# A hybrid diffusion step with top-2 experts: inner tile and position bias moved from TensorE to VectorE, block bounds read inside the blocks

## The chip, the cores and the metric

The kernel runs on one core of one Trainium2 chip. The time is the device time of one execution in microseconds. Before the change the median of three runs is 1415.07 us (1414.96 to 1417.32).

## The reference, cut to what matters

Two layers work on 128 context tokens and 256 latent tokens of width 1024. Layer 0 mixes tokens by differential attention, layer 1 by neighbourhood attention: each latent token sees 16 columns of 64 in the rows of its grid (4 rows here), with a learned bias by relative position, and all 128 context keys. After each attention every token goes through two of 32 experts, chosen by its own scores.

```python
s_nb = einsum('bqhd,biqjhd->bhqij', q_r, k_nb) * scale + bias      # layer 1, latent tokens
s = concatenate([s_nb.reshape(B, H, GRID_W, kh * kw), s_ctx], -1)
p = softmax(s, -1)
...
def one_block(args):                                               # experts, both layers
    tok, e, w = args
    xb = xt[tok]
    hb = silu(xb @ w_gate[e]) * (xb @ w_up[e])                     # 1024 -> 512
    return (hb @ w_down[e]) * w[:, None]                           # 512 -> 1024
```

## The kernel before

All is fp32. The order of the work on each engine is written out by hand, with semaphores between the engines.

**Experts.** Tokens are sorted into blocks of 32 of one expert each. The layers have 73 such blocks together (TensorE works on 77, the last ones of a layer being fillers). An expert's weights are six pieces of 1 MB: four of gate and up (pieces 0 to 3), two of down (4 and 5). The ring `ring` holds three experts. The SP queue (`load`, L361 to L384) loads expert after expert; from the fourth on, each piece waits until TensorE has read the piece of the expert three before it for the last time (`taken`: `gu_used`, `dn_used`), and until the same piece of the expert before has landed (`moe_land`).

A block with 32 tokens uses the array in four groups of 32 columns. In `gate_up` (L1072) group j takes the tokens as weights and, as moving data, columns j x 128 to j x 128 + 127 of w_gate and of w_up, so partition group j of the PSUM bank holds the hidden columns of that run for the 32 tokens, gate beside up (W = 256). ScalarE takes Silu of the gate half (`sg`, L755), VectorE multiplies by the up half (`hp`, L1555). For the down products the hidden index has to stand on partitions: TensorE transposes hp (128x128, L1090) to PSUM, and ScalarE copies it to `hm` (L758). In `down` (L1092) each of four 32-column pieces of hm is the weight for four column groups of w_down (WD = 256 columns each). VectorE copies the result to `yo` (L1563), and GpSimd stores it by an indirect DMA (L560). GpSimd also gathers the tokens of the block two ahead (L547) into `xg`, which VectorE turns into `xs` by its blockwise transpose (L1550), in every body after hp and ahead of the copy to yo.

TensorE's loop (L1106 to L1115) runs over triples of experts, with three inner loops over the blocks of one expert. Each inner loop's bounds, `first` and `end`, are read from the table `tabi` in SBUF into registers by `table` (L298) just ahead of it.

**Attention of layer 1.** A unit u is one tile of 128 queries and one pair of heads, 24 units, the first eight the context tile (128 keys, no bias), sixteen latent (384 keys: 128 context, 256 latent). `scores` (L905) puts both heads' scores into two PSUM banks; for latent units TensorE then adds the bias to the last 256 columns, by a product of the identity with the table `btab` (L919). VectorE's `maxima` (L1273) takes the negated maximum over all keys of both heads; ScalarE's `exps` (L695) takes the exponentials with that as bias and sums them; VectorE's `normalise` (L1316) divides; TensorE transposes the probabilities (L930); ScalarE copies these (`take_pT`, L708); TensorE multiplies by the values (`attend`, L934); VectorE takes the output (`take_oT`, L1325). TensorE's order in a turn is transposes of u, scores of u + 3, attend of u - 1; VectorE's is maxima of u + 1, normalise of u, output of u - 2; ScalarE's is exponentials of u + 2, copy of u. The mask of the 16-column window is added to btab by VectorE in twelve steps (L1267) while the projections run, and TensorE waits for the twelve ahead of its first transposes of this stage (L879).

## Time and profile before

| | us |
|---|---|
| median of the runs | 1415.07 |
| the profiled execution's own time | 1414.9 |
| its span, first to last instruction | 1413.1 |
| TensorE busy (matmul) | 1083.7 |
| VectorE busy | 401.0 |
| ScalarE busy | 180.4 |
| GpSimd busy | 255.4 |

The profile is of one execution on one core. Its times count from the start of the span. TensorE's matmuls are pipelined and their ends are modelled, so a following group can start up to 0.2 us before the one ahead of it ends; weight loads (PEld) run beside them. Reading registers from a table, branches and semaphores are not counted as busy. `[1.07 <-issue]` is idle time ended by nothing that the profile shows. PEclk is TensorE's granted clock: 1.00 is 2.4 GHz, 0.50 is 1.2 GHz. The mean granted clock over the span was 0.895.

The stages in the profile: layer 0's projections, attention and routing to about 378 us, its experts to 717, layer 1's projections to 886, its attention to 971, output projection, norm and routing to 1038, its experts to 1370.

### The profile page before, as it was taken

The page shows a single profiled execution, that of the slowest core. Times are in us where ns is not written, and L with a number is a line of the kernel's source. Part 1 is how long each engine was busy: PE and PEld are TensorE (multiplying, and loading weights), DVE is VectorE, ACT ScalarE, POOL GpSimd, SP SyncE. Part 2 cuts the span into 40 slices and gives each one's busy share as a digit, 9 for nine tenths or more (in the row PEclk, how much of TensorE's full clock was granted, in tenths as well). Part 3 has the DMA queues.
Part 4 walks back from the last instruction along what each step waited for, and adds up shares of the span by engine and source line. Part 5 has one row for each costly group of instructions (what it writes and reads, how often), then busy time and mean ns, then how long its engine had stood idle before and what let it go on. Part 6 is the DMA issues. An engine that isn't in the chain of part 4 may idle for free.

```text
span 1413.1 us, 26713 instructions
## 1 busy us (share of the span) xinstructions
PE 1083.7 (77%) x9857; PEld 561.9 (40%) x9858; DVE 401.0 (28%) x965; ACT 180.4 (13%) x485; POOL 255.4 (18%) x450
## 2 busy tenths in 40 slices
PE   5899998798687786656557999899837657788781
PEld 1333344544344443323223444565434323444440
DVE  0120217768411111001035002565871001111117
ACT  0110026400000000000012000552000000000000
POOL 2000002201133333212102010000022212333230
PEclk9999998897599999877787999899958878999996
DMA  9866892107979999999965993201079999999932
GB/s 367 305 239 262 332 358 86 60 18 257 415 319 387 414 415 414 415 415 416 416 267 126 113 160 117 75 1 60 30 298 413 412 415 417 415 379 389 414 112 109
DMA packets 85414, 389.76 MB, mean 276 GB/s; under 512 B 17612, under 2 KB 18124, under 8 KB 57720
## 3 DMA queue, kind: packets, MB, share of 16 engines
q1 hardware_dynamic: 63136, 349.77, 63.4%
q0 software_dynamic: 15200, 36.74, 9.6%
q10 hardware_dynamic: 7032, 2.68, 0.7%
q8 instruction: 24, 0.39, 0.1%
q14 instruction: 22, 0.18, 0.0%
HBM read 379.66 MB, written 17.44 MB: 281 GB/s over the span
## 4 chain that ended last, share of the span: by engine, by line
DMA 41%; PE 34%; issue 9%; DVE 9%; ACT 2%; DVEq 1%; POOLq 1%; SPq 1%; POOL 0%; ACTq 0%; PEldq 0%
DMA ring<-in_w_down_dram 36%; PE ps L824 15%; PE ps L1083 5%; PE ps L985 3%; PE ps L1101 3%; DMA ring<-in_w_ada_dram 2%; PE ps L800 1%; PE ps L930 1%; PE ps L912 1%; PE ps L919 1%; PE ps L952 1%; POOLq L457 1%; DVEq L1123 1%; DMA qkv<-ybuf 1%; DVE o L1201 1%
## 5 line engine op out<-in xcount | busy, mean ns | idle before, releaser
L1083 PE MATMUL ps<-ring,xs 128*32 128x256 f32 x4928 | 316.5, 411 | 115.0 <-DMA ring<-in_w_up_dram 75.1
L1083 PEld LDWEIGHTS ps<-ring,xs 128*32 128x32 f32 x4928 | 181.5, 117 | 242.7 <-issue 162.1
L824 PE MATMUL ps<-ring,hT 128*128 128x512 f32 x576 | 254.7, 601 | 8.1 <-ACT hT L648 4.3
L1101 PE MATMUL ps<-ring,hm 128*32 128x256 f32 x2464 | 158.7, 399 | 31.2 <-ACT hm L758 26.8
L824 PEld LDWEIGHTS ps<-ring,hT 128*128 128x128 f32 x576 | 109.6, 193 | 152.2 <-issue 141.9
L1555 DVE TENSOR_TENSOR hp<-sg,ps 128x128 f32<-128x128 f32 x73 | 21.0, 288 | 379.2 <-ACT sg L755 379.2
L1101 PEld LDWEIGHTS ps<-ring,hm 128*32 128x32 f32 x2464 | 73.6, 113 | 91.7 <-ACT hm L758 41.1
L547 POOL DMA_INDIRECT xg<-xmod,idx x77 | 80.8, 1050 | 66.0 <-POOL idx L545 63.9
L755 ACT ACTIVATE sg<-ps 128x128 f32<-128x128 f32 x73 | 20.2, 277 | 553.2 <-PE ps L1083 553.2
L560 POOL DMA_INDIRECT ybuf<-yo,idy x73 | 75.1, 1029 | 64.4 <-POOL idy L557 64.4
L985 PE MATMUL ps<-ring,qT 128*128 128x512 f32 x192 | 85.0, 603 | 2.2 <-DVE qT L1366 1.8
L1563 DVE COPY yo<-ps 128x256 f32<-128x256 f32 x73 | 31.0, 424 | 188.2 <-PE ps L1101 188.2
L557 POOL COPY idy<-rowi 128x1 int32 (+1 forms) x73 | 13.2, 181 | 344.7 <-DVE yo L1563 330.5
L800 PE MATMUL ps<-ring,cond 128*32 128x512 f32 x384 | 56.5, 707 | 17.5 <-DMA ring<-in_w_ada_dram 17.5
L1090 PE MATMUL ps<-cst,hp 128*128 128x128 f32 x77 | 25.9, 336 | 52.2 <-DVE hp L1555 50.7
L985 PEld LDWEIGHTS ps<-ring,qT 128*128 128x128 f32 x192 | 36.8, 194 | 47.9 <-issue 45.1
L704 ACT ACTIVATE hT<-ps,negm 128x384 f32<-128x384 f32 (+1 forms) x96 | 48.0, 505 | 54.5 <-DVE negm L1279 49.1
L1090 PEld LDWEIGHTS ps<-cst,hp 128*128 128x128 f32 x77 | 10.9, 141 | 91.9 <-DVE hp L1555 90.2
L686 ACT ACTIVATE qkv<-ps 128x1024 f32<-128x1024 f32 x18 | 18.4, 1023 | 220.4 <-PE ps L824 220.4
L912 PE MATMUL ps<-kT,qT 64*128 64x384 f32 (+1 forms) x192 | 42.3, 526 | 4.0 <-ACT hT L704 2.3
L930 PE MATMUL ps<-cst,hT 128*128 128x128 f32 x168 | 31.1, 304 | 12.1 <-DVE hT L1289 8.9
L1279 DVE TENSOR_REDUCE negm<-ps 128x2 f32<-128x768 f32 (+1 forms) x48 | 36.9, 773 | 4.5 <-PE ps L912 4.3
(269 smaller groups left out, 838.0 us busy)
## 6 DMA issues: line engine op xcount, KB each, us to landing
ring<-in_w_gate_dram SPq DMA_DIRECT2D x82, 1024.0 KB, 15.0
ring<-in_w_up_dram SPq DMA_DIRECT2D x82, 1024.0 KB, 15.5
ring<-in_w_down_dram SPq DMA_DIRECT2D x82, 1024.0 KB, 15.9
ring<-in_w_ada_dram SPq DMA_DIRECT2D x48, 1024.0 KB, 8.2
ring<-in_w_qkv_a_dram SPq DMA_DIRECT2D x12, 1024.0 KB, 5.3
ring<-in_w_qkv_b_dram SPq DMA_DIRECT2D x12, 1024.0 KB, 15.2
modb<-mdram POOLq DMA_DIRECT2D x12, 512.0 KB, 8.8
qkv<-ybuf SPq DMA_DIRECT2D x6, 1024.0 KB, 8.3
```

Of the source, the lines that this page charges most:

```text
L547: pool.indirect_dma_start(out=xg[:, lane, :], out_offset=None, in_=xmod.rearrange("r (j w) -> (r j) w", j=G), in_offset=bass.IndirectOffse ...
L560: pool.indirect_dma_start(out=ybuf.rearrange("r (j w) -> (r j) w", j=G), out_offset=bass.IndirectOffsetOnAxis(ap=at, axis=0), in_=yo[:, la ...
L704: ins = act.activation(e[:, h, 0:n], ps[:, 2 * (u % 2) + h, 0:n], ACT.Exp, bias=negm[:, u % 2, h:h + 1], accum_out=sums[:, t % 2, h, u % P ...
L800: ins = mm(ps[j * BLK:(j + 1) * BLK, ADA_BANK[i], :], cond[:, k, :], raw[:, n % RING, j * 512:(j + 1) * 512], start=(k == 0), stop=(k == K ...
L824: ins = mm(ps[:, 2 * t + hf, :], lhs[:, k, t * P:(t + 1) * P], raw[:, slot, kk * D + hf * 512:kk * D + (hf + 1) * 512], start=(k == 0), st ...
L912: ins = mm(ps[:, 2 * (u % 2) + h, 0:keys[t]], qT[HD * h:HD * (h + 1), j, t * P:(t + 1) * P], kT[HD * h:HD * (h + 1), j, key0[t]:key0[t] + ...
L930: ins = nc.tensor.transpose(ps[:, 4 + (u % 2 if l == 0 else h), i * P:(i + 1) * P], prob[u % 2][:, h, i * P:(i + 1) * P], ident)
L985: ins = mm(ps[:, 2 * t + hf, :], oT[:, k, t * P:(t + 1) * P], raw[:, n % RING, kk * D + hf * 512:kk * D + (hf + 1) * 512], start=(k == 0), ...
L1083: ins = mm(ps[j * BLK:(j + 1) * BLK, 1, 0:W].rearrange("p (a n) -> p a n", a=2), xs[:, k, :], w[:, :, at:at + FW], start=(k == 0), stop=(k ...
L1090: nc.tensor.transpose(ps[:, 3, 0:P], hp[:, :], ident).then_inc(ht_done[l], 1)
L1101: ins = mm(ps[j * BLK:(j + 1) * BLK, 5, 0:WD], hm[:, 2 * c + q, :], ring[:, slot + GU + c, q * D + j * WD:q * D + (j + 1) * WD], start=(c ...
L1279: v.tensor_reduce(negm[:, u % 2, :], sc[:, :, 0:n], AX, ALU.max, negate=True).then_inc(negm_rdy[l], 1)
```

## The change

1. In `gate_up` group j now takes, from each run of 128 columns (f = 0 to 3), the 32 columns f x 128 + 32 j onwards, of gate and of up, so the moving data are eight runs of 32 columns in place of two of 128. The products, their number and the columns per product stay. With this mapping the 128x128 tile hp needs only its sixteen 32x32 blocks turned, each in place, to be the hm of the down products. VectorE does that with its blockwise transpose from SBUF to SBUF, behind a drain. TensorE's transpose, ScalarE's copy and two semaphores go.
2. For latent units of layer 1 TensorE no longer adds the bias. `maxima` takes the maximum over the 128 context columns of both heads into `most`, then, for each head, one instruction adds the bias to the 256 latent columns in PSUM and takes their maximum together with that of the context columns; a small step negates both. Between these stand drains.
3. TensorE no longer waits for the masks; VectorE, which writes them, has a drain behind them.
4. The loop bounds of an expert are carried in registers: `lo` and `hi` are set before the loops, and in every block, between gate_up and down, the end of the next expert is read from the table into `after`. Behind an inner loop two register moves take the place of the two reads.

```diff
...
@@ -246,7 +247,7 @@
         idx_rdy, idy_rdy = sem2("idx_rdy"), sem2("idy_rdy")
         gath = [[sem(f"gath{l}_{i}") for i in range(LANES)] for l in range(LAYERS)]
         y_wr = [[sem(f"y_wr{l}_{i}") for i in range(LANES)] for l in range(LAYERS)]
-        xs_rdy, hp_rdy, ht_done, sg_rdy, hm_rdy = sem2("xs_rdy"), sem2("hp_rdy"), sem2("ht_done"), sem2("sg_rdy"), sem2("hm_rdy")
+        xs_rdy, sg_rdy, hm_rdy = sem2("xs_rdy"), sem2("sg_rdy"), sem2("hm_rdy")
         yo_rdy = sem2("yo_rdy")
         pool_steps, sp_steps = sem("pool_steps"), sem("sp_steps")
         sq_done, sq_rdy, hn_rdy = sem("sq_done"), sem("sq_rdy"), sem("hn_rdy")
...
@@ -754,16 +755,9 @@
                     act.wait_ge(gu_used[l], read_up(b))
                     act.activation(sg[:, :], ps[:, 1, 0:FW], ACT.Silu).then_inc(sg_rdy[l], 1)
-                    act.wait_ge(ht_done[l], b + 1)
-                    act.activation(hm[:, :, :], ps[:, 3, 0:P].rearrange("p (j n) -> p j n", j=G), ACT.Copy)\
-                        .then_inc(hm_rdy[l], 1)
-
                 body(0)
                 with act.Fori(1, n_blk) as b:
                     body(b)
-
-                act.wait_ge(dn_used[l], n_blk * 2 + 2)
-                act.sem_inc(hm_rdy[l], BUFS - 1)
                 for t in range(NT):
                     act.wait_ge(yg_ld[l][t], 16)
...
@@ -875,8 +871,6 @@
                 if l == 0:
                     pe.wait_ge(roped, 4)
                     pe.wait_ge(mblk_ev, 5)
-                else:
-                    pe.wait_ge(bias_rdy, 12)
                 pe.wait_ge(qkv_ev[l], 9)
                 pe.wait_ge(ctx_ld[l], 32)
                 for j in range(PAIRS):
...
@@ -907,17 +901,10 @@
                     if u >= 2:
                         pe.wait_ge(exp_done[l], u - 1)
-                    biased = l == 1 and t > 0
                     for h in range(2):
                         ins = mm(ps[:, 2 * (u % 2) + h, 0:keys[t]],
                                  qT[HD * h:HD * (h + 1), j, t * P:(t + 1) * P],
-                                 kT[HD * h:HD * (h + 1), j, key0[t]:key0[t] + keys[t]], start=True, stop=not biased)
-                    if biased:
-                        m0 = (2 - 2 * (t - 1)) * GRID_W
-                        for h in range(2):
-                            at = (2 * j + h) * BM * GRID_W + m0
-                            ins = mm(ps[:, 2 * (u % 2) + h, P:keys[t]], ident, btab[:, at:at + ROWS * GRID_W],
-                                     start=False, stop=True)
+                                 kT[HD * h:HD * (h + 1), j, key0[t]:key0[t] + keys[t]], start=True, stop=True)
                     ins.then_inc(sc_done[l], 1)
                 def transpose_prob(u):
...
@@ -1068,6 +1055,8 @@
                 pe.wait_ge(tab_rdy, l + 1)
                 pe.wait_ge(tok_rdy, l + 1)
                 n_trip = table(pe, T_TRIP, 1, (NE + BUFS) // BUFS)
+                pe.reg_mov(lo, 0)
+                pe.reg_mov(hi, table(pe, T_CUM + 2, 1, NB + BUFS - 1))
                 def gate_up(b, slot, landed):
...
@@ -1079,15 +1068,11 @@
                         for kk in range(4):
                             k = 4 * half + kk
                             for j in range(G):
-                                at = kk * DE + j * FW
-                                ins = mm(ps[j * BLK:(j + 1) * BLK, 1, 0:W].rearrange("p (a n) -> p a n", a=2), xs[:, k, :],
-                                         w[:, :, at:at + FW], start=(k == 0), stop=(k == KD - 1))
+                                ins = mm(ps[j * BLK:(j + 1) * BLK, 1, 0:W].rearrange("p (a f n) -> p a f n", a=2, f=G),
+                                         xs[:, k, :],
+                                         w[:, :, kk * DE:(kk + 1) * DE].rearrange("p a (f j n) -> p a f j n", f=G, j=G)
+                                         [:, :, :, j, :], start=(k == 0), stop=(k == KD - 1))
                         ins.then_inc(gu_used[l], 1)
-
-                def transpose_h(b):
-
-                    pe.wait_ge(hp_rdy[l], b + 1)
-                    nc.tensor.transpose(ps[:, 3, 0:P], hp[:, :], ident).then_inc(ht_done[l], 1)
                 def down(b, slot, landed):
...
@@ -1107,12 +1092,12 @@
                     for turn in range(BUFS):
                         at = trip * BUFS + turn
                         landed = at * 16 + 16
-                        first = table(pe, T_CUM + 1 + at, 0, NB)
-                        end = table(pe, T_CUM + 2 + at, 1, NB + BUFS - 1)
-                        with pe.Fori(first, end) as b:
+                        with pe.Fori(lo, hi) as b:
                             gate_up(b, BASE[turn], landed)
-                            transpose_h(b)
+                            pe.reg_mov(after, table(pe, T_CUM + 3 + at, 0, NB + BUFS - 1))
                             down(b, BASE[turn], landed)
+                        pe.reg_mov(lo, hi)
+                        pe.reg_mov(hi, after)
         @block.vector
         def _(dve):
...
@@ -1265,7 +1250,8 @@
                     for f in range(12):
                         part = btab[:, f * 512:(f + 1) * 512].rearrange("p (a n) -> p a n", n=GRID_W)
                         v.tensor_tensor(part, part, cst[:, C_WIN:C_WIN + GRID_W].unsqueeze(1).to_broadcast([P, 8, GRID_W]),
-                                        ALU.add).then_inc(bias_rdy, 1)
+                                        ALU.add)
+                    dve.drain()
                 for j in range(PAIRS):
                     dve.wait_ge(qk_ps[l], 2 * j + 2)
                     v.tensor_copy(kT[:, j, :], ps[:, 5 + 2 * (j % 2), :]).then_inc(kT_ev[l], 1)
...
@@ -1276,7 +1262,17 @@
                     n = keys[t]
                     sc = ps[:, 2 * (u % 2):2 * (u % 2) + 2, :]
                     dve.wait_ge(sc_done[l], u + 1)
-                    v.tensor_reduce(negm[:, u % 2, :], sc[:, :, 0:n], AX, ALU.max, negate=True).then_inc(negm_rdy[l], 1)
+                    if l == 0 or t == 0:
+                        v.tensor_reduce(negm[:, u % 2, :], sc[:, :, 0:n], AX, ALU.max, negate=True).then_inc(negm_rdy[l], 1)
+                        return
+                    m0 = (2 - 2 * (t - 1)) * GRID_W
+                    chain(v.tensor_reduce(most[:, 0:2], sc[:, :, 0:P], AX, ALU.max))
+                    for h in range(2):
+                        at = (2 * j + h) * BM * GRID_W + m0
+                        v.tensor_tensor_reduce(sc[:, h, P:n], sc[:, h, P:n], btab[:, at:at + ROWS * GRID_W], 1.0,
+                                               most[:, h:h + 1], ALU.add, ALU.max, most[:, 2 + h:3 + h])
+                    dve.drain()
+                    v.tensor_scalar(negm[:, u % 2, :], most[:, 2:4], -1.0, None, ALU.mult).then_inc(negm_rdy[l], 1)
                 def combine(u):
                     t, j = u // PAIRS, u % PAIRS
...
@@ -1552,7 +1548,8 @@
                 def hidden(b):
                     dve.wait_ge(sg_rdy[l], b + 1)
-                    v.tensor_tensor(hp[:, :], sg[:, :], ps[:, 1, FW:W], ALU.mult).then_inc(hp_rdy[l], 1)
+                    chain(v.tensor_tensor(hp[:, :], sg[:, :], ps[:, 1, FW:W], ALU.mult))
+                    v.transpose(hm[:, :, :].rearrange("p f n -> p (f n)"), hp[:, :]).then_inc(hm_rdy[l], 1)
                 def take_y(b, lane, turn):
...
@@ -1582,7 +1579,7 @@
                 dve.drain()
                 dve.sem_inc(xs_rdy[l], BUFS - 2)
-                dve.sem_inc(hp_rdy[l], BUFS - 1)
+                dve.sem_inc(hm_rdy[l], BUFS - 1)
                 dve.sem_inc(yo_rdy[l], BUFS - 2)
                 take_experts(l, 0)
```

TensorE, layer 0, one expert's loop over its blocks: before, the two table reads (`TENSOR_LOAD tabi`) stand ahead of the loop, and a transpose (L1090) between gate_up (L1083) and down (L1101), which follows.

```order
L300 TENSOR_LOAD tabi
L300 ISA x3
L300 TENSOR_LOAD tabi
L300 ISA x2
L1112 UNCONDITIONAL_BRANCH
L1112 ISA
L1077 ISA [waits xs_rdy_0]
L1083 MATMUL ps<-ring,xs 32x256 [waits moe_land0_1,moe_land0_0]
L1083 MATMUL ps<-ring,xs 32x256 x15
L1083 MATMUL ps<-ring,xs 32x256 [waits moe_land0_3,moe_land0_2]
L1083 MATMUL ps<-ring,xs 32x256 x15
L1090 MATMUL ps<-cst,hp 128x128 [waits hp_rdy_0]
```

The same place of the changed kernel (gate_up is L1071, down L1086).

```order
L1095 UNCONDITIONAL_BRANCH
L1095 ISA
L1066 ISA [waits xs_rdy_0]
L1071 MATMUL ps<-ring,xs 32x256 [waits moe_land0_1,moe_land0_0]
L1071 MATMUL ps<-ring,xs 32x256 x15
L1071 MATMUL ps<-ring,xs 32x256 [waits moe_land0_3,moe_land0_2]
L1071 MATMUL ps<-ring,xs 32x256 x15
L301 ISA
L301 TENSOR_LOAD tabi
L301 ISA x2
L1086 MATMUL ps<-ring,hm 32x256 [waits moe_land0_4,yo_rdy_0,hm_rdy_0]
```

One table read has moved from the loop's head into the block, ahead of the down products, the other is gone, and so is the transpose.

VectorE, one latent unit of layer 1's attention (`sc_done_1` counts TensorE's scores), before.

```order
L1279 TENSOR_REDUCE negm<-ps 128x2 [waits sc_done_1]
L1322 RECIPROCAL rsum<-sums 128x2 [waits exp_done_1]
L1323 TENSOR_TENSOR hT<-hT,rsum 128x768
L1329 COPY qT<-ps 128x128 [waits pv_done_1]
L1279 TENSOR_REDUCE negm<-ps 128x2 [waits sc_done_1]
```

The same of the changed kernel; the combined step is shown as ISA, followed by the one that writes its maximum.

```order
L1269 TENSOR_REDUCE most<-ps 128x2 [waits sc_done_1]
L1272 ISA ps,most<-ps,btab,most 128x256
L1272 ISA most 128x1
L1272 ISA ps,most<-ps,btab,most 128x256
L1272 ISA most 128x1
L1275 TENSOR_SCALAR negm<-most 128x2
L1318 RECIPROCAL rsum<-sums 128x2 [waits exp_done_1]
L1319 TENSOR_TENSOR hT<-hT,rsum 128x768
L1325 COPY qT<-ps 128x128 [waits pv_done_1]
```

Five instructions more stand between the scores' arrival and the step that lets ScalarE take the exponentials; the rest of the unit keeps its order.

## Rows read from the trace of the kernel before

**Rows 1.** The page's slices (40 of 35.3 us each): what the DMA engines moved, GB/s.

```profile
GB/s 367 305 239 262 332 358 86 60 18 257 415 319 387 414 415 414 415 415 416 416 267 126 113 160 117 75 1 60 30 298 413 412 415 417 415 379 389 414 112 109
```

**Rows 2.** The page's chain that ended last: shares of the span by line.

```profile
DMA ring<-in_w_down_dram 36%; PE ps L824 15%; PE ps L1083 5%; PE ps L985 3%; PE ps L1101 3%; DMA ring<-in_w_ada_dram 2%; PE ps L800 1%; PE ps L930 1%; PE ps L912 1%; PE ps L919 1%; PE ps L952 1%; POOLq L457 1%; DVEq L1123 1%; DMA qkv<-ybuf 1%; DVE o L1201 1%
```

**Rows 3.** Windows, layer 1: busy PE, PEld, DVE, ACT, POOL; PEclk, DMA share, GB/s.

```profile
1244.00:1248.00 4.00, 4.00 (x80) 2.40 (x76) 0.42 (x1) 0.00 (x0) 1.20 (x2) 1.00 0.55 216
1248.00:1252.00 4.00, 2.90 (x45) 1.21 (x37) 0.67 (x2) 0.56 (x2) 1.26 (x3) 1.00 0.92 301
1296.00:1300.00 4.00, 3.28 (x61) 1.77 (x53) 0.66 (x3) 0.28 (x1) 1.80 (x4) 1.00 0.69 212
```

**Rows 4.** Timeline of the SP queue (start, us, engine, line): w_gate loads after a standstill.

```profile
424.38 0.36 SPq L384 DMA_DIRECT2D ring<-in_w_gate_dram  x1
1247.32 0.36 SPq L384 DMA_DIRECT2D ring<-in_w_gate_dram  x1
```

**Rows 5.** Timeline of TensorE in the experts (start, us, what, [idle before <- releaser]).

```profile
378.78 5.30 PE L1083 MATMUL ps<-ring,xs 128*32 128x256 f32 x64 [11.35 <-DVE xs L1550]
401.67 3.66 PE L1083 MATMUL ps<-ring,xs 128*32 128x256 f32 x64 [0.63 <-DMA ring<-in_w_gate_dram]
422.08 3.64 PE L1083 MATMUL ps<-ring,xs 128*32 128x256 f32 x64
...
1216.90 1.07 PE L1101 MATMUL ps<-ring,hm 128*32 128x256 f32 x16 [0.66 <-DMA ring<-in_w_down_dram]
1333.13 1.07 PE L1101 MATMUL ps<-ring,hm 128*32 128x256 f32 x16 [0.59 <-DMA ring<-in_w_down_dram]
1362.49 3.66 PE L1083 MATMUL ps<-ring,xs 128*32 128x256 f32 x64 [1.07 <-issue]
```

**Rows 6.** Chain of waits in layer 1's attention, two units: the bias products.

```profile
932.98 1.06 PE ps L919 x4
...
936.50 1.06 PE ps L919 x4
```

**Rows 7.** Timeline of VectorE in the same stage: the idle time of a unit.

```profile
931.38 0.29 DVE L1329 COPY qT<-ps 128x128 f32<-128x128 f32 x1 [1.25 <-PE ps L952]
```

**Rows 8.** Timeline of all engines in one expert block, from hp to down.

```profile
485.54 0.29 DVE L1555 TENSOR_TENSOR hp<-sg,ps 128x128 f32<-128x128 f32 x1 [3.34 <-ACT sg L755]
485.76 0.45 DVE L1550 STREAM_TRANSPOSE xs<-xg 128x256 f32<-128x256 f32 x1
485.88 0.33 PE L1090 MATMUL ps<-cst,hp 128*128 128x128 f32 x1 [0.72 <-DVE hp L1555]
486.25 0.28 ACT L758 ACTIVATE hm<-ps 128x128 f32<-128x128 f32 x1 [0.74 <-PE ps L1090]
486.58 1.93 PE L1101 MATMUL ps<-ring,hm 128*32 128x256 f32 x32 [0.37 <-ACT hm L758]
```

**Rows 9.** Groups of VectorE: a drained step of one column (busy, mean ns | idle before).

```profile
L1169 DVE SCALAR_TENSOR_TENSOR newt<-newt,var 128x1 f32<-128x1 f32 x8 | 1.3, 160 | 0.6
```

**Rows 10.** Groups in the window of layer 1's attention, shapes kept apart.

```profile
L1279 DVE TENSOR_REDUCE negm<-ps 128x2 f32<-128x768 f32 x16 | 15.2, 947 | 0.0
L1323 DVE TENSOR_TENSOR hT<-hT,rsum 128x256 f32<-128x256 f32 x3 | 1.3, 424 | 0.2
L1279 DVE TENSOR_REDUCE negm<-ps 128x2 f32<-128x256 f32 x2 | 0.8, 414 | 0.0
```

**Rows 11.** TensorE's clock: a window of the attention, and down products after a wait.

```profile
898.00:911.00 13.00, 12.40 (x55) 6.83 (x54) 5.72 (x20) 6.48 (x30) 0.00 (x0) 0.50 0.00 0
...
1184.08 3.64 PE L1101 MATMUL ps<-ring,hm 128*32 128x256 f32 x32 [0.37 <-ACT hm L758]
```

**Rows 12.** Timeline of ScalarE: exponentials of two successive units.

```profile
918.65 0.58 ACT L704 ACTIVATE hT<-ps,negm 128x384 f32<-128x384 f32 x1 [1.42 <-DVE negm L1279]
...
921.74 0.58 ACT L704 ACTIVATE hT<-ps,negm 128x384 f32<-128x384 f32 x1 [1.15 <-DVE negm L1279]
```

**Rows 13.** Timeline of VectorE: the mask added to the bias table.

```profile
853.92 7.32 DVE L1267 TENSOR_TENSOR btab<-btab,cst 128x512 f32<-128x512 f32 x12 [89.31 <-DMA btab<-bpad]
```

4 lines of the change are left out of this document (3 added, 1 removed).

## The prediction

> **What bounds the kernel now.** I read the slices of the page first. From the eleventh to the twentieth slice (layer 0's experts) and from the thirty-first to the thirty-eighth (layer 1's) the DMA engines move about 414 GB/s [rows 1]. The two slices from 389 to 459 us fall short of it (319 and 387), and so do the two from 1237 to 1307 (379 and 389). The chain of waits says the same: the expert weights' last piece alone holds 36% of the span [rows 2]. So most of the expert time is a stream of weights at full rate, in which a faster block is worth nothing. What a block can win is where the stream stood still, and behind the last load.
>
> The stream stands still where three experts are in the ring and the next load waits until TensorE has read the oldest one for the last time. The windows show it around 1246 (216 and 301 GB/s in 4 us each) and around 1298 (212) [rows 3]. The SP queue shows who ends it: the w_gate loads after a standstill, at 424.38 and 1247.32 [rows 4], are issued when TensorE is in the last gate and up products of a large expert (the first 2.3 us after they began at 422.08 [rows 5]). Elsewhere the queue is refilled in time.
>
> In layer 1's attention the DMA is silent, and one unit follows the other every 3.52 us (932.98 to 936.50) [rows 6]. TensorE is without a gap there, while VectorE stands idle for 1.25 us of each unit [rows 7]. TensorE bounds this stage.
>
> **The expert block.** Today VectorE's product hp starts at 485.54 and takes 0.29 to 485.83; TensorE turns it (0.33), ScalarE copies it (0.28), and the down products start at 486.58, 0.75 after hp ended [rows 8]. The change puts a drain and one VectorE transpose of 128x128 in place of both. A drained step costs 0.16 and 0.07 idle (0.6 over 8) [rows 9]. The transpose of 128x256 takes 0.45 [rows 8]; VectorE's maximum costs 0.95 over 768 columns and 0.41 over 256 [rows 10], so 1.04 ns a column, and the 128x128 transpose is 0.45 - 0.13 = 0.32. Then 0.07 + 0.32 + 0.05 for the semaphore (485.83 to 485.88) = 0.44, and a block is 0.31 shorter. From both sides: with the transpose at 0.16 (the smallest VectorE step) it is 0.47, with it at the whole 0.45 it is 0.18. What is queued behind it: the next block's xs transpose comes 0.4 later, but is needed only after the 1.93 of down products, so it stays hidden.
>
> The Trainium skill, "VectorE: DVE Perf Modes", section "The three transpose paths", gives 311 ns for VectorE's blockwise turn and 390 ns for TensorE's, both of 128x128 bf16. With 0.31 in place of my 0.32 the sum would stay as it is.
>
> **The block bounds.** Where TensorE goes from one expert to the next it reads two table entries, and stands idle for 0.6 us (0.63 at 401.67), or 1.07 where the outer loop turns too (1362.49) [rows 5]; between blocks of one expert there is no gap. I take the 0.6 and 0.1 of lost overlap, 0.7 a change of expert, as saved, and leave the outer loop's rest. The read that comes in its place stands between gate/up and down, once per block. There TensorE waits for hm anyway, 1.11 us by the new count (0.72 + 0.33 + 0.37 today, less 0.31). Two reads and the loop's branches cost at most about 0.7 more than the sequencer's lead, so one fits below 1.11 even if it starts only when the products end. Cost: nothing; uncovered it would cost up to 0.7 a block.
>
> **What of it reaches the end.** Layer 0: the stream resumes at 424.38, and TensorE's start at 378.78 is set by the gather. Between lie seven blocks, so six shortened gaps and one change of expert (401.67): 6 x 0.31 + 0.7 = 2.6 us, all of which passes on, because the stream is full from there to the end of the layer. The two slices lack (95 + 27) / 414 x 35.3 = 10 us, so the idle time is not used up. Layer 1: the large expert whose first down waits for a load until 1216.90 [rows 5] has five more blocks; the load at 1247.32 comes four gaps earlier, 1.2. The second standstill cost (414 - 212) x 4 / 414 = 2.0; by then TensorE has won some eleven gaps and three changes (5.5), so it vanishes. The stream ends 3.2 earlier. Then TensorE has the rest: from the down at 1333.13, which waits for its load, four blocks and the last expert's one follow, five gaps and one change: 5 x 0.31 + 0.7 = 2.3. Layer 1: 5.5; both layers 8.1. Against it I set 0.8 for the clock: with TensorE ahead, it waits longer before the expert of 1333.13, and after such a wait a set of down products took 3.64 in place of 1.93 at 1184.08 [rows 11], 1.7 with a chance of about a half. Experts: 7.3.
>
> **The gate and up products** read the same 256 columns in eight runs of 32 where they were two of 128. No row shows runs of 32; going from one run of 256 (down: 1.93 for 32 products) to two of 128 (3.64 for 64) cost nothing [rows 5, 8]. I take nothing; the upper bound is a slowdown as of the rival below.
>
> **The position bias.** TensorE loses the four L919 pieces a unit, 1.06 [rows 6], and would need 2.46 a unit. VectorE today needs 3.52 - 1.25 = 2.27, of it 0.95 for the maximum over 768 columns [rows 10]. In its place come a maximum over 256 (0.41), a drain (0.07), two combined add-and-maximum steps of 256 columns at the 0.42 of an element-wise step of that size, their two accumulator reads, a drain (0.07) and a step of two columns (0.16). For the reads no row of VectorE exists: between nothing and 0.16 each; I take 0.08, since small steps partly overlap. Sum 1.71, so VectorE needs 3.03 a unit (2.9 to 3.2). A third bound appears: ScalarE's exponentials, its copy, TensorE's turning of the copy's successor and again the exponentials form a ring, which set the pace at the start of the stage: 918.65 to 921.74, 3.09 us [rows 12]. So 3.10 a unit, and 0.42 saved in each of the eleven steps from the thirteenth unit's exponentials to the last's: 4.6. The first biased unit also loses its bias products at half clock (0.50 until 911 [rows 11]); about 0.9 of it reaches ScalarE. Attention: 5.5. The rest follows serially (gates loaded after the last unit, fold, norm) and moves up whole. The masks are added to btab at 853.92 for 7.3 us [rows 13], well before the attention (its window of rows 11 begins at 898), so TensorE's lost wait on them is worth nothing.
>
> The Trainium skill, "VectorE: DVE Perf Modes", section "Two Vector instructions with no wait between them", says that an operation that also writes out its accumulator is two instructions; the order of the changed kernel shows the same pairs. "Vector Engine (DVE) Microarchitecture Reference", section "Points that are easy to get wrong", says that a combined step with two sources in SBUF runs at half rate. Here one source is in PSUM; if the rule held all the same, the time would be that of rival A.
>
> **Sum.** 1414.9 of the profiled execution (span 1413.1), less 7.3 and 5.5: 1402.1. The runs' median is 1415.07, 0.2 above it; I say 1402.
>
> **Rivals.**
> A. The add-and-maximum runs at half rate (0.27 more each). VectorE then needs 3.57 a unit, attention wins nothing, and only the experts do: 1407.6. For it: no row has VectorE writing PSUM. Against it: the maximum reads PSUM and pays 1.04 ns a column. Chance 0.14.
> B. The experts win nothing, since a later wait takes it all (gathers, the queue), attention does: 1409.4. Against it: the standstills have TensorE as their only releaser. Chance 0.07.
> C, the other side. Gate and up are slower by the short runs. About 23 blocks lie where TensorE sets the time (7, 11 and 5). The gains of 12.8 are used up when a block's 3.5 grow by 0.56, 16%. At 25% it is 0.88 x 23 = 20 less 12.8: 1422. For it: the pattern is new to this kernel. Against it: two runs cost no more than one. Chance 0.08. The Trainium skill, "Advanced Engine Details and Errata", section "SBUF Cachelines", wants only that successive accesses share a 16-byte line; runs of 128 bytes do, so by it C is out. No run here shows it yet.
> D. The table read isn't covered and costs each block 0.4 to 0.7: 23 x 0.55 = 12.7, no gain from the blocks: 1415. Chance 0.05.
> My forecast has 0.66.
>
> **Numbers.** The forecast's own range: attention between 3.5 and 8 (the pace between 2.93 and 3.25), experts between 4 and 11 (gap 0.18 to 0.47, clock nothing or 1.7): 1397 to 1407. With A and B inside, the range is 1396 to 1411, which leaves out C, D and a little of the ends. About 0.2%, 3 us, is what a measurement can tell here. Faster by more: the forecast, A, B: 0.88 with something of D; same: 0.04 (D and the near edge of C); slower: 0.08.
>
> **What would show it.** Down products start 0.44 after hp ends, on TensorE no gap over 0.1 between experts; exponentials of successive biased units 3.1 apart, with VectorE without idle time; the standstill at 1298 gone, the others shorter; gate and up still 3.64. The forecast is wrong if the accumulating step takes 0.7, if gate and up exceed 4, or if the stream's restart in layer 0 is not 2.6 us earlier against the first block.

## The result, and the profile after

The changed kernel takes 1407.79 us (median of five runs, 1406.43 to 1408.54), the kernel before 1415.07 (five runs, 1414.16 to 1417.41). The ratio over the runs is 0.9937, 95% interval 0.9925 to 0.9949. The medians are 7.3 us apart (a ratio of 0.9949, the small end of the interval), where 13 were forecast. The time lies in the stated range (1396 to 1411), above the predicted 1402. The profiled execution took 1406.97 (span 1405.2, mean granted clock 0.872 where it was 0.895).

The page's slices, with the granted clock in tenths and what the DMA engines moved:

```profile
PEclk9999997998599999757677999899959868999896
...
GB/s 369 291 250 269 312 361 108 57 19 255 416 329 404 415 415 414 415 416 416 414 262 135 131 160 101 75 1 61 30 301 412 415 414 416 415 377 414 414 107 110
```

Against [rows 1] the two slices from 389 us are up from 319 and 387 to 329 and 404. In layer 1 the slice that had 389 now has 414, so one of its two standstills is gone; the other slice is unchanged (379, 377).

The chain that ended last, shares of the span by line, against [rows 2]:

```profile
DMA ring<-in_w_up_dram 21%; PE ps L820 15%; DMA ring<-in_w_down_dram 13%; PE ps L1071 7%; PE ps L1086 4%; PE ps L972 3%; DMA ring<-in_w_ada_dram 2%; PE ps L796 1%; DVEq L1108 1%; POOLq L458 1%; DMA qkv<-ybuf 1%; PE ps L917 1%; PE ps L905 1%; PE ps L939 1%; DVE ps L1272 1%
```

The stream of weights still holds a third of the span (21% and 13%). TensorE is now so early that it waits for w_up, an earlier piece of an expert than w_down. Gate and up are L1071 now, down L1086.

One block on all engines, against [rows 8]:

```profile
486.45 0.29 DVE L1551 TENSOR_TENSOR hp<-sg,ps 128x128 f32<-128x128 f32 x1 [3.34 <-ACT sg L756]
...
486.81 0.31 DVE L1552 STREAM_TRANSPOSE hm<-hp 128x128 f32<-128x128 f32 x1
487.05 0.44 DVE L1546 STREAM_TRANSPOSE xs<-xg 128x256 f32<-128x256 f32 x1
...
487.18 1.93 PE L1086 MATMUL ps<-ring,hm 128*32 128x256 f32 x32 [1.10 <-DVE hm L1552]
```

From the end of hp (486.74) to down it is 0.44, as forecast. TensorE across the first change of expert in layer 0, against [rows 5]:

```profile
392.18 3.64 PE L1071 MATMUL ps<-ring,xs 128*32 128x256 f32 x64
396.92 1.93 PE L1086 MATMUL ps<-ring,hm 128*32 128x256 f32 x32 [1.10 <-DVE hm L1552]
398.67 3.64 PE L1071 MATMUL ps<-ring,xs 128*32 128x256 f32 x64
```

Block follows block every 6.49 us (392.18 to 398.67), 6.80 before, and the idle time at a change of expert is gone altogether. Gate and up still take 3.64 with the runs of 32 columns. Every local price of the expert part was right.

Where the 7.3 us appear, as the shift of the same event between the two traces:

| event | before | after | shift |
|---|---|---|---|
| first expert block of layer 0 | 378.78 | 377.47 | -1.31 |
| the load that resumes the stream, layer 0 | 424.38 | 420.66 | -3.72 |
| last store's copy, layer 0 | 717.97 | 714.53 | -3.44 |
| layer 1's first maxima | 895.44 | 893.36 | -2.08 |
| first expert load of layer 1 | 1035.65 | 1029.63 | -6.02 |
| the load that resumes the stream, layer 1 | 1247.32 | 1241.67 | -5.65 |
| last store's copy, layer 1 | 1369.56 | 1362.03 | -7.53 |
| span | 1413.1 | 1405.2 | -7.9 |

None of the work ahead of the first event is edited. The start of layer 0's attention, which only unedited work precedes, lies between 211.6 and 214.8 us in the thirteen traces of this case. So one trace's first stages differ by up to 3 us for no reason that the edits give, and stage shifts are to be trusted to about 1 us, totals only as medians.

Attention gave 3.9 (from -2.08 to -6.02). The experts gave 2.4 at the resume of layer 0 and then lost 1.6 of it before attention began; in layer 1 they gave 1.5 in this trace.

For layer 1's experts even 1 us is too fine. The changed kernel's expert code also runs in experts_only and oT_late below, which differ from it only in attention, and with added matmuls in gap_fill, copy_first and change_fill. From the first expert load of layer 1 to the last store's copy:

| kernel | us | against before |
|---|---|---|
| before | 333.9 | |
| changed | 332.4 | -1.5 |
| experts_only (same expert code) | 329.7 | -4.3 |
| oT_late (same expert code) | 330.2 | -3.7 |
| gap_fill (filler in each block) | 330.4 | -3.6 |
| copy_first (filler in each block) | 329.6 | -4.3 |
| change_fill (filler at each change of expert) | 332.9 | -1.0 |

### The profile page after: what moved, and what is told of

Its sections match the earlier page's. It is cut to its first block, busy times and chain, and to the rows that moved or that the text cites. A ratio compares the mean times of both kernels' runs of the same rounds, so it can differ in the third digit from the quotient of the medians.

```text
span 1405.2 us, 26607 instructions
## 1 busy us (share of the span) xinstructions
PE 1056.9 (75%) x9716; PEld 536.0 (38%) x9717; DVE 432.2 (31%) x1118; ACT 160.3 (11%) x412; POOL 255.9 (18%) x450
## 4 chain that ended last, share of the span: by engine, by line
DMA 38%; PE 34%; DVE 11%; issue 10%; ACT 3%; DVEq 2%; POOLq 1%; SPq 1%; POOL 0%; ACTq 0%; PEldq 0%
DMA ring<-in_w_up_dram 21%; PE ps L820 15%; DMA ring<-in_w_down_dram 13%; PE ps L1071 7%; PE ps L1086 4%; PE ps L972 3%; DMA ring<-in_w_ada_dram 2%; PE ps L796 1%; DVEq L1108 1%; POOLq L458 1%; DMA qkv<-ybuf 1%; PE ps L917 1%; PE ps L905 1%; PE ps L939 1%; DVE ps L1272 1%
## 5 line engine op out<-in xcount | busy, mean ns | idle before, releaser
L1071 PE MATMUL ps<-ring,xs 128*32 128x256 f32 x4928 | 330.5, 424 | 109.6 <-DMA ring<-in_w_up_dram 89.1
L1071 PEld LDWEIGHTS ps<-ring,xs 128*32 128x32 f32 x4928 | 177.5, 120 | 250.6 <-issue 166.8
L1086 PE MATMUL ps<-ring,hm 128*32 128x256 f32 x2464 | 167.3, 415 | 87.4 <-DVE hm L1552 79.8
L1086 PEld LDWEIGHTS ps<-ring,hm 128*32 128x32 f32 x2464 | 75.9, 116 | 178.4 <-DVE hm L1552 119.6
L705 ACT ACTIVATE hT<-ps,negm 128x384 f32<-128x384 f32 (+1 forms) x96 | 48.0, 506 | 50.6 <-DVE negm L1266 22.3
L917 PE MATMUL ps<-cst,hT 128*128 128x128 f32 x168 | 30.5, 301 | 23.9 <-ACT hT L718 15.6
L905 PE MATMUL ps<-kT,qT 64*128 64x384 f32 (+1 forms) x192 | 43.4, 539 | 4.0 <-ACT hT L705 2.3
L1257 DVE COPY kT<-ps 128x512 f32<-128x512 f32 x16 | 11.1, 692 | 94.4 <-PE ps L887 93.8
L1546 DVE STREAM_TRANSPOSE xs<-xg 128x256 f32<-128x256 f32 x75 | 32.7, 436 | 5.5 <-DMA xg<-xmod,idx 5.5
L917 PEld LDWEIGHTS ps<-cst,hT 128*128 128x128 f32 x168 | 19.6, 150 | 32.0 <-DVE hT L1319 14.9
```

The costliest lines, as they stand in the source:

```text
L705: ins = act.activation(e[:, h, 0:n], ps[:, 2 * (u % 2) + h, 0:n], ACT.Exp, bias=negm[:, u % 2, h:h + 1], accum_out=sums[:, t % 2, h, u % P ...
L905: ins = mm(ps[:, 2 * (u % 2) + h, 0:keys[t]], qT[HD * h:HD * (h + 1), j, t * P:(t + 1) * P], kT[HD * h:HD * (h + 1), j, key0[t]:key0[t] + ...
L917: ins = nc.tensor.transpose(ps[:, 4 + (u % 2 if l == 0 else h), i * P:(i + 1) * P], prob[u % 2][:, h, i * P:(i + 1) * P], ident)
L1071: ins = mm(ps[j * BLK:(j + 1) * BLK, 1, 0:W].rearrange("p (a f n) -> p a f n", a=2, f=G), xs[:, k, :], w[:, :, kk * DE:(kk + 1) * DE].rear ...
L1086: ins = mm(ps[j * BLK:(j + 1) * BLK, 5, 0:WD], hm[:, 2 * c + q, :], ring[:, slot + GU + c, q * D + j * WD:q * D + (j + 1) * WD], start=(c ...
L1546: v.transpose(xs[:, :, :].rearrange("p k n -> p (k n)"), xg[:, lane, :]).then_inc(xs_rdy[l], 1)
```

## The experiments

Each of the first three makes one part of the change alone, from the kernel before. Ratios are to the kernel before, measured beside each run.

**turn_only**

```diff
+ v.transpose(hm, hp).then_inc(hm_rdy[l], 1)      # VectorE, for TensorE's transpose and ScalarE's copy
+ w[...]"p a (f j n) -> p a f j n"[:, :, :, j, :]  # gate/up in runs of 32
```

> The kernel before with one part of the change: the inner tile is turned by VectorE, and gate and up are read in runs of 32; bias and block bounds stay as they were. Theory 1 (TensorE's half clock after waits for weights takes back what the shorter gap wins in layer 1): 6 x 0.31 less 0.5 of cold blocks in layer 0, some 1.5 in layer 1, so 3 us: 1412. Rival 1 (the gain of the experts was counted too high from the start, the resume of the stream in layer 1 never moves): only layer 0's 1.9: 1413. Rival 2 (each part brings what the prediction gave it, and only together they lose): 1.9 + 3.6 = 5.5: 1409.6. The standstill at 1298 shall be gone or shorter in theory 1 and rival 2.

Measured 1412.19 us (11 runs), ratio 0.9979 (0.9970 to 0.9988): 3.2 less than the kernel before measured beside it (1415.37), as theory 1 has it. Rival 2 (1409.6) is out for this part. Rival 1 (1413) lies inside the interval, but its mechanism doesn't fit the trace: the load that resumes the stream in layer 1 comes 210.3 us behind the stage's first load (1034.48 to 1244.73) where it was 211.7, and the slice of the second standstill has 408 GB/s against 389.

**bias_only**

```diff
- mm(ps[...], ident, btab[...], start=False, stop=True)
+ v.tensor_tensor_reduce(sc[:, h, P:n], sc[:, h, P:n], btab[...], 1.0, most[:, h:h+1], ALU.add, ALU.max, most[...])
```

> The kernel before with the bias added by VectorE alone; experts as they were. Theory 2 (attention is held by a ring through VectorE's take of the output, which stands ahead of the next maxima, and TensorE's attend behind the scores): a pair of units takes 6.60 us again, attention wins 3.9 and all of it reaches the end: 1411.2. Rival (the ring is VectorE's work alone and was only disturbed by other parts): 3.03 a unit, 5.5: 1409.6.

Measured 1413.06 (11 runs, 1410.09 to 1416.76), ratio 0.9983 (0.9974 to 0.9992): 2.3 less, under both expectations. In its trace the way from the first maxima to the first expert load is 135.5 us (898.23 to 1033.71) against 140.2 before, so 4.7 are gained there; that trace began layer 0's attention 2.7 later than before's (214.38, 211.71). The pace is theory 2's: two units take 6.59 in the chain of waits (transposes of probabilities at 922.31 and 928.90). Why the median keeps only half of the stage's gain stays open.

**bounds_only**

```diff
  transpose_h(b)
+ pe.reg_mov(after, table(pe, T_CUM + 3 + at, 0, NB + BUFS - 1))
  down(b, BASE[turn], landed)
```

> The kernel before with only the block bounds held in registers. Idle time of 0.6 us between two experts goes in places where TensorE sets the time: one in layer 0, some three to four in layer 1. Theory 1: 0.7 in layer 0, 1 in layer 1 after the clock's share: 1413.4. Rival 2 (each part brings what the prediction gave it): 0.7 + 2.1: 1412.3. A rival that the read costs as much inside the block: 1415.

Measured 1419.89 (6 runs), ratio 1.0031 (1.0019 to 1.0043): 4.5 slower. The last rival named the direction, a read that costs inside the block, but not the size (1415). TensorE's timeline in layer 0:

```profile
386.17 3.66 PE L1087 MATMUL ps<-ring,xs 128*32 128x256 f32 x64
390.54 0.33 PE L1094 MATMUL ps<-cst,hp 128*128 128x128 f32 x1 [0.71 <-DVE hp L1560]
391.52 1.93 PE L1105 MATMUL ps<-ring,hm 128*32 128x256 f32 x32 [0.65 <-ACT hm L758]
393.24 3.66 PE L1087 MATMUL ps<-ring,xs 128*32 128x256 f32 x64
```

A block takes 7.07 us. Down starts 0.65 behind the transpose where it was 0.37: the read stands behind the transpose and outlasts ScalarE's copy. That it is taken up only when the transpose has been issued is a reading which the next run tests. The releaser that is printed, ACT, was done 0.34 earlier (its copy ran from 390.90 to 391.18). In the 23 blocks where the prediction has TensorE set the time, 0.27 each would be 6.2 us.

**bounds_early** moves the read ahead of the wait.

```diff
+ pe.reg_mov(after, table(pe, T_CUM + 3 + at, 0, NB + BUFS - 1))
  transpose_h(b)
- pe.reg_mov(after, table(pe, T_CUM + 3 + at, 0, NB + BUFS - 1))
```

> The kernel before with only the block bounds in registers, as in bounds_only, but the table entry is read ahead of TensorE's wait for hp and not behind its transpose. If the read was what made a block 0.27 longer there (7.07 in place of 6.80), because it began only when the transpose had been issued, it is now hidden in the 0.72 of that wait: blocks of 6.80, no gap between experts, and 1413 (0.7 to 2.7 below the kernel before). Rival (a read inside the block costs wherever it stands): 7.07 again and 1420.

Measured 1413.74 (10 runs), before 1415.63, ratio 0.9984 (0.9969 to 0.9999). TensorE, the same stage:

```profile
394.08 3.64 PE L1087 MATMUL ps<-ring,xs 128*32 128x256 f32 x64
...
399.13 1.93 PE L1105 MATMUL ps<-ring,hm 128*32 128x256 f32 x32 [0.37 <-ACT hm L758]
400.88 3.64 PE L1087 MATMUL ps<-ring,xs 128*32 128x256 f32 x64
```

6.80 a block, no gap at the change of expert (400.88). So the read is free where a wait of TensorE covers it, and one place further down it costs 6 us in all (1419.89 against 1413.74).

**experts_only** is turn and bounds together, without the bias part (both diffs above; the read stands between gate_up and down, as in the changed kernel).

> The changed kernel without its bias part: inner tile turned by VectorE and block bounds in registers, bias still by TensorE. turn_only took 3 us off and bounds_early 2. Theory 1 (the two add up in layer 0, where the stream's resume follows TensorE, and what layer 1 wins meets the stream and the clock): 4.8 less in the experts, 1410.6. Rival (the parts are worth more together, as the forecast of 7.3 for both had it): 1408. Rival (the half clock after the longer waits takes back what the second part adds): 1412, as turn_only.

Measured 1410.29 (6 runs), before 1414.80, ratio 0.9958 (0.9942 to 0.9973): 4.5 by the medians, theory 1's number. The interval reaches from 3.8 to 8.2 us, so the forecast's 7.3 is not ruled out; the rival at 1412 is. turn_only and bounds_early alone gave 3.2 and 1.9, within the intervals the same.

The trace says more. Its first maxima of layer 0 come at 214.30, 2.6 later than before's, and from there to the end it is 7.0 us shorter. And at the first standstill of layer 1 its products run at full clock, where the changed kernel's own trace has half clock at the same place. First the changed kernel:

```profile
1210.84 1.94 PE L1086 MATMUL ps<-ring,hm 128*32 128x256 f32 x16 [1.38 <-DMA ring<-in_w_down_dram]
1212.54 4.27 PE L1071 MATMUL ps<-ring,xs 128*32 128x256 f32 x64
```

And experts_only:

```profile
1216.13 1.07 PE L1094 MATMUL ps<-ring,hm 128*32 128x256 f32 x16 [0.96 <-DMA ring<-in_w_down_dram]
1217.02 3.64 PE L1079 MATMUL ps<-ring,xs 128*32 128x256 f32 x64
```

Here the stream resumes 1.4 earlier against the stage's first load (210.3 for 211.7), for the four gaps of the forecast (1.2).

**light_before** and **light_after** thin out the stream of weights: in layer 1, from the fourth expert on, they leave out half of each piece, so their results are wrong and only their times are of use.

```diff
+ if l == 1 and freed is not None:
+     src, dst = src[:, 0:2, :], dst[:, 0:2, :]      # w_down: 0:1
```

> The kernel before, but in layer 1 the loads from the fourth expert on bring half of each piece (half of the weights are left out), so that the stream of weights cannot bound these experts. TensorE then sets the time there: about 36 blocks of 6.80 and some 17 changes of expert of 0.6 to 1.07, in place of the 334 us from the first load to the last store. Some 270 us, so a time near 1350. It is the base for light_after.

> The changed kernel with the same half loads in layer 1. Theory 1 (the change's gain in TensorE's own time is whole, 0.31 a block and 0.6 to 1.07 a change of expert; in the full kernel the stream and the clock after its waits cover it): the experts of layer 1 take 36 x 0.31 + 17 x 0.65 = 22 us less than in light_before, and with 3 of layer 0 and 4 of attention the whole is 29 us less. The granted clock is the same in both. Rival (TensorE's longer idle time per block lowers the clock also without waits for weights, or the gathers hold the blocks): less than 12 us in layer 1.

One execution each: 1375.13 and 1342.33 us. From layer 1's first expert load to its last store's copy it is 296.3 (1033.27 to 1329.53) and 268.7 (1028.64 to 1297.31): 27.6 less, even more than the 22 of theory 1. One part of the surplus is that the changes of expert with 1.07 of idle time were counted at 0.65; the rest is not traced. The stream isn't gone everywhere: until about 1130 TensorE of light_after still waits for weights (1.60 at 1113.28). One window of light_after (busy PE, PEld, DVE, ACT, POOL; granted clock, DMA share, GB/s):

```profile
1160.00:1200.00 40.00, 33.36 (x604) 18.74 (x596) 8.41 (x25) 1.67 (x6) 14.82 (x24) 1.00 0.39 140
```

The clock is full with the longer idle time in each block, as it is in light_before. The rival (the idle time in a block lowers the clock, or the gathers hold the blocks) is out. In layer 1 the expert part is worth 28 us with half the weights and 1.5 to 4.3 with all of them: there the stream sets most of the time.

**oT_late**, from the changed kernel. A chain of waits over two units of attention in the changed kernel:

```profile
930.93 0.85 PE ps L917 x6
931.78 0.85 PE ps L905 x4
932.63 0.83 PE ps L939 x12
...
933.48 0.29 DVE qT L1325
...
934.22 0.49 DVE ps L1272
...
935.25 0.18 DVE negm L1275
...
935.93 0.76 ACT hT L705 x3
936.69 0.71 ACT hT L718
...
937.53 0.85 PE ps L917 x6
```

It comes back to the transposes of probabilities (L917) after 6.60 us, 3.30 a unit. Read it as a ring: transposes, scores (L905), attend (L939) on TensorE; then VectorE's take of the attended output (L1325), which stands ahead of the next maximum and add (L1272); exponentials (L705), copy (L718). Every second unit VectorE stands idle for attend:

```profile
926.88 0.29 DVE L1325 COPY qT<-ps 128x128 f32<-128x128 f32 x1 [0.54 <-PE ps L939]
```

The edit puts one unit between attend and take:

```diff
- if u >= 2: take_oT(u - 2)
+ if u >= 3: take_oT(u - 3)
```

> The changed kernel, with VectorE taking the output of a unit one unit later (unit u-3 behind the normalising of unit u), so that the next maxima never wait for attend. Theory 2 (ring through take of the output and attend): the alternation 3.57/3.03 goes, the pace comes to VectorE's own 3.03 to 3.10, 16 units x 0.25 = 3 to 4 us less than the changed kernel's 1407.8: 1404. Rival (ScalarE's copy of the transposed probabilities and TensorE's transposes set the pace): still 3.30 a unit, 1407.8. Rival (attend then waits for the bank of the output): 3.5 a unit, 1411.

Measured 1402.04 (4 runs), ratio to before 0.9909 (0.9894 to 0.9924). By the medians that is 5.8 less than the changed kernel; by the two ratios (0.9937, 0.9909) it is 4.0, as theory 2 has it. The same view:

```profile
932.98 0.86 PE ps L917 x6
...
934.41 0.76 ACT hT L705 x3
935.16 0.71 ACT hT L718
...
936.01 0.86 PE ps L917 x6
```

3.03 a unit; L905, L939 and VectorE have left the chain. What is left is transposes, exponentials and copy, the third bound of the prediction: it is real, and 3.03 here. VectorE goes through a unit in 2.95 until it has caught up, near 931, and is then held to 3.03 too. First maxima to first expert load is 132.0 us (136.3 in the changed kernel), 4.3 less; the rest of the 5.8 is no gain of this edit that could be shown, since it lies in layer 1's experts (330.2 for 332.4 with the same code). Theory 2 is shown, and both rivals, as they gave their pace (3.30 and 3.5), are out.

**copy_first**, from gap_fill below: in layer 1 ScalarE copies the transposed probabilities of a unit before the exponentials of the next but one.

```diff
+ if l == 1: take_pT(u)
  exps(u + 2)
- take_pT(u)
```

> gap_fill, with ScalarE in layer 1's attention copying the transposed probabilities of unit u before the exponentials of unit u+2 and not behind them. In oT_late the chain of waits runs through TensorE's transposes (0.86), the exponentials (0.76) and the copy (0.71), 3.03 a unit, beside VectorE's 2.95. Theory 2 (with take of the output out of the way VectorE is next): the exponentials leave the ring, the pace falls to VectorE's 2.95, 16 x 0.08 = 1 us: 1399, hardly to be told from gap_fill's 1400.1. Rival (VectorE then waits for exponentials that come 0.8 later, in its normalising): 3.2 a unit and more, 1403. Rival (the pace was never ScalarE's): 1400.1.

Measured 1398.27 (4 runs), ratio to before 0.9883 (0.9867 to 0.9900). ScalarE's exponentials:

```profile
920.04 0.58 ACT L705 ACTIVATE hT<-ps,negm 128x384 f32<-128x384 f32 x1
...
922.99 0.58 ACT L705 ACTIVATE hT<-ps,negm 128x384 f32<-128x384 f32 x1
```

2.95 a unit: VectorE is the bound at last. First maxima to first expert load is 130.0 us, where gap_fill's trace has 131.8. In the medians the step from gap_fill is not told apart, the intervals overlap. It is the fastest version here, 16 us under its before (1414.30) and 9.5 under the changed kernel.

**gap_fill** and **change_fill** go after the clock. TensorE in the tail of layer 1, changed kernel:

```profile
1310.48 1.07 PE L1086 MATMUL ps<-ring,hm 128*32 128x256 f32 x16 [0.56 <-DMA ring<-in_w_down_dram]
1316.20 3.60 PE L1071 MATMUL ps<-ring,xs 128*32 128x256 f32 x32 [4.66 <-DMA ring<-in_w_up_dram]
1321.79 2.46 PE L1071 MATMUL ps<-ring,xs 128*32 128x256 f32 x32 [1.98 <-DMA ring<-in_w_up_dram]
1325.33 3.64 PE L1086 MATMUL ps<-ring,hm 128*32 128x256 f32 x32 [1.08 <-DVE hm L1552]
1328.75 4.19 PE L1071 MATMUL ps<-ring,xs 128*32 128x256 f32 x64
1334.05 1.93 PE L1086 MATMUL ps<-ring,hm 128*32 128x256 f32 x32 [1.11 <-DVE hm L1552]
```

And its windows there:

```profile
1312.00:1316.00 4.00, 0.00 (x0) 0.00 (x0) 0.04 (x1) 0.00 (x0) 1.99 (x4) 1.00 1.02 418
1316.00:1320.00 4.00, 3.60 (x32) 1.69 (x32) 0.00 (x0) 0.00 (x0) 0.47 (x1) 0.57 1.01 408
...
1324.00:1328.00 4.00, 2.92 (x32) 1.23 (x32) 0.96 (x3) 0.28 (x1) 0.00 (x0) 0.50 1.02 422
```

TensorE is ahead of the stream, stands idle for 4.66 us, and then runs at half clock (0.50 is the 1.2 GHz level). From 1321.79, when the last w_up has landed, to the down products at 1334.05 it takes 12.3; at the durations of the full clock (3.0 to the down products, 1.75 to the next gate products, 4.74 to their down) it would be 9.5. In the kernel before TensorE had no such wait, [rows 5] shows 0.59 at 1333.13.

gap_fill, from oT_late:

```diff
  ins.then_inc(gu_used[l], 1)                 # gate and up
+ for j in range(G): mm(ps[..., 3, 0:W], cst[...], cst[:, 0:W], start=True, stop=True)
  pe.wait_ge(hm_rdy[l], b + 1)
```

> oT_late (the changed kernel with VectorE's take of the output one unit later) with four matmuls into an unused bank between the gate and up products and the wait for hm, 0.5 us of the 1.1 that TensorE waits there (at half clock 1.0). Nothing else changes. Theory 1 (the lost time is half clock after waits for weights): TensorE is back at full clock sooner, the cold blocks at 1211 and at 1325 (down 3.64 in place of 1.93) get shorter, up to 2 us of gain over oT_late: 1400. Rival (the clock falls with the wait and these 0.5 us change nothing): 1402, as oT_late. Rival (the added matmuls delay hm's reader): 36 x some tenths where TensorE bounds, 1405.

Measured 1400.07 (6 runs), ratio to before 0.9879 (0.9857 to 0.9902), beside oT_late's 0.9909 (0.9894 to 0.9924): the intervals overlap. The granted clock from 430 to 690 us rose from 0.84 to 0.89, and from 690 to 720 from 0.62 to 0.77. But from layer 0's first maxima to the end its trace is as long as oT_late's (1186.2 both). Its tail:

```profile
1313.07 3.64 PE L1071 MATMUL ps<-ring,xs 128*32 128x256 f32 x32 [4.65 <-DMA ring<-in_w_up_dram]
1318.62 3.35 PE L1071 MATMUL ps<-ring,xs 128*32 128x256 f32 x32 [1.91 <-DMA ring<-in_w_up_dram]
...
1323.07 1.93 PE L1088 MATMUL ps<-ring,hm 128*32 128x256 f32 x32 [0.67 <-DVE hm L1555]
```

Down is at 1.93 here, but so it was in oT_late's trace (1321.89). The added matmuls delay nothing; a gain is not shown.

change_fill, from oT_late:

```diff
+ pe.wait_ge(moe_land[l][0], landed)
+ for _ in range(2):
+     for j in range(G): mm(ps[..., 3, 0:W], cst[...], cst[:, 0:W], start=True, stop=True)
  with pe.Fori(lo, hi) as b:
```

> oT_late with eight matmuls into an unused bank at each change of expert, once its first piece (gate) has landed and before the wait for the second: 1.0 us at full clock, 1.9 at half. Where TensorE waits for weights they lie in a wait of 2 to 3.7 us. Theory 1 (what the shortened blocks lose in the tail is half clock): behind them, at the last expert's wait near 1312, the first 32 gate and up products take 1.9 to 2.8 in place of 3.64, and the last store comes 1 to 2 us sooner against its load; each change of expert where TensorE does not wait costs 1.0, one in layer 0 and some four in layer 1, so the whole is 1402 to 1405, no faster than oT_late. Rival (the clock stays at half until the real products have run as long as before): 3.64 again at that place, and 1405 to 1407.

Measured 1403.64 (6 runs, 1402.00 to 1407.90), ratio to before 0.9913 (0.9897 to 0.9928). The tail:

```profile
1316.35 1.05 PE L1098 MATMUL ps<-cst 128*32 128x256 f32 x16
1317.21 1.91 PE L1071 MATMUL ps<-ring,xs 128*32 128x256 f32 x32
1321.32 1.93 PE L1071 MATMUL ps<-ring,xs 128*32 128x256 f32 x32 [2.20 <-DMA ring<-in_w_up_dram]
...
1326.85 1.93 PE L1086 MATMUL ps<-ring,hm 128*32 128x256 f32 x16 [1.43 <-DMA ring<-in_w_down_dram]
1328.56 4.23 PE L1071 MATMUL ps<-ring,xs 128*32 128x256 f32 x64
```

The two halves of gate and up take 1.9, as theory 1 said. But each unhidden filler cost TensorE its 0.86, so it came to this expert later (1317.21), and the waits are shorter: the test is not clean. Half clock then comes two steps later (16 down products 1.93 for 1.07, the next 64 products 4.23 for 3.64). The last store's copy is at 1362.84, no sooner.

## Why the prediction was right or wrong

**The number first.** 1407.79 is 0.8 above the forecast's own range (1397 to 1407). It is inside the stated range only because that was stretched for rivals A and B, and it falls on A's 1407.6 by luck: A had attention win nothing and the experts 7.3, and attention did win 3.9.

**The block, the bounds, the gate and up products: right.** 0.44 from hp to down, 6.49 a block, the transpose 0.31 for my 0.32, gate and up 3.64. The read is hidden, since TensorE waits 1.10 there; that this hangs on the place is what bounds_only showed. At a change of expert all of the idle time went, also the outer loop's 1.07. Rivals C and D are out, and so is B, since experts_only is faster (ratio 0.9958). The rule that I cited from the Trainium skill ("Advanced Engine Details and Errata", "SBUF Cachelines"), by which the runs of 32 should cost nothing, agrees with the trace (3.64 in runs of 128 and in runs of 32).

**Layer 0: right at the resume, given back behind it.** The stream resumes 2.41 earlier against the first block, forecast 2.6. To the end of the experts nearly all of it passes on, as forecast: from the resuming load to the last store's copy it is 293.9 us, 293.6 before. TensorE's waits for pieces are longer, though, and the granted clock from 430 to 690 is 0.84 where it was 0.91, from 690 to 720 0.63 for 0.78. What is lost is lost behind the experts: 0.5 ahead of the transposes of the next norm (743.30 for 746.23) and 0.9 in the projections. TensorE had been idle for 18.5 us there, 15.1 before, but that this is the cause isn't shown. Layer 1's attention starts 0.8 earlier by the change, not 2.6.

**Layer 1's experts: the step "against it I set 0.8 for the clock" was too small for the changed kernel's trace, and not for all.** Half clock took back 1.5 at 1210.84 and 1212.54 (16 down products 1.94 for 1.07, 64 products 4.27 for 3.64; the rows stand at experts_only), so the first standstill did not shrink: its window has 148 GB/s, and its load comes 5.65 earlier for 6.02 at the stage's start. The windows around the two standstills:

```profile
1240.00:1244.00 4.00, 2.89 (x56) 1.53 (x52) 0.75 (x3) 0.28 (x1) 2.19 (x4) 1.00 0.57 148
...
1292.00:1296.00 4.00, 2.89 (x56) 1.55 (x52) 0.80 (x3) 0.28 (x1) 2.24 (x4) 1.00 1.02 419
```

The second is gone, as forecast, and worth its 2.0. In the tail the clock took 2.8, more than the 2.3 that the five gaps and the change of expert were to bring. I had the mechanism, at one place and at half its chance. How often it strikes is not settled: with the same expert code experts_only runs the first place at full clock, and its stage is 4.3 shorter than before's, near the 4.7 that the forecast leaves for layer 1 if the whole 0.8 is set against it. That these pieces run at half clock is read off the rows; that the whole missing gain is the clock's was not shown, since neither filler gave it back. light_before and light_after show only that it isn't lost in the blocks.

**Attention: the step "so 3.10 a unit" failed.** VectorE's own 3.03 came out (2.95 in oT_late), with the add-and-maximum at 0.49 and starting every 0.41, so rival A is out. One prices an engine by its sum, and I did, and looked for a ring through ScalarE and TensorE. I left out that VectorE's queue is in order: take of the output, which waits for attend, stands ahead of the next maxima. That was harmless while TensorE was the bound, for attend was then always done. The ring gave 3.30 (3.03 and 3.57 by turns), attention 3.9 for 5.5. oT_late shows it by taking it away: what then bounds is the very ring that I had found, at 3.03.

The Trainium skill's rule on accumulators ("VectorE: DVE Perf Modes", "Two Vector instructions with no wait between them") agrees with the trace: the read is an instruction of its own, with a row of 0.14. VectorE's timeline in the changed kernel:

```profile
928.02 0.14 DVE L1272 DVE_READ_ACCUMULATOR2_ANT most<- 128x1 f32 x1
928.02 0.49 DVE L1272 CUSTOM_DVE_ANT_0 ps<-ps,btab,most 128x256 f32<-128x256 f32 x1
```

The next step starts together with the read, so the read costs nothing between the two; I had 0.08.

**The sum.** By medians the experts gave 4.5 (experts_only) for 7.3, and the bias on top of them 2.5 (1410.29 to 1407.79) for 5.5. The traces give more. Counted from layer 0's first maxima to the end, which leaves out the unedited start, they are shorter than before's by 3.7 (turn_only), 4.1 (bias_only), 7.0 (experts_only) and 8.7 us (changed kernel), one trace each. That the medians show less, as in bias_only, is not explained. Of the 1.6 that attention fell short the ring is the shown cause; for the experts the shortfall lies between 0.3 and 2.8, and its cause stays open.

## What to carry to other kernels

When work goes from the bounding engine to another, walk through the receiving engine's queue in order: an instruction that waited for the old bound without ever being late can close a ring with it, and moving it one iteration back is free (4.3 us in the attention stage here, more than the 3.9 that the change itself won there). A value read on an engine's own queue is free only ahead of a wait that was there anyway; behind it, it cost 0.27 a block. And where a stream of weights bounds, a faster consumer buys the shorter standstills and the tail, and can pay in both with a lower clock (1.5 and 2.8 us in the changed kernel's trace, nothing at the first place in experts_only's): price its cold restarts at every longer wait, and read the stage in more than one trace.

## What the runs showed of the hardware that was not expected

- A filler of 0.6 us in each block's wait (gap_fill) raised the granted clock from 0.84 to 0.89 over 260 us in which the stream bounds, and the time from the resuming load to the last store's copy did not change (294.1 us, 293.9 in oT_late).
- The clock did not fall through idle time of 1.1 us in every block of 6.49 (granted 1.00 from 1160 to 1200 in light_after). Behind the changed kernel's wait of 4.66 us for weights it was down (0.57, then 0.50 in the windows above). One place with shorter waits went both ways: half clock behind 3.39, 1.17 and 1.38 us of idle time in the changed kernel (1205.28 to 1210.84), full clock behind 1.87, 1.10 and 0.96 in experts_only (1211.06 to 1216.13).
- An instruction that is queued behind a matmul and reads a register from SBUF shows up in no row: its time is printed as idle time whose releaser is another engine (0.65 for 0.37).
